# Moving the first fold, the late gate-tile subtractions, one expert store and the score sign in a two-layer diffusion backbone

## What is computed

```python
# two of three mixers
z = v                                            # hyena: short convolution first, then twice
for o, gate in enumerate((x1, x2)):
    z = gate * bidirectional_long_conv(z, h_spec[:, o], skip[o])
# neighbourhood attention, 8 heads of 64
s_lat = einsum(q_rot, k_rot) * scale + bias      # bias = -1e30 outside the column window
s_ctx = einsum(q_plain, k_ctx) * scale
p = softmax(concatenate([s_lat, s_ctx]))
# experts (top 2 of 16)
out = sum_e gates[:, e] * (silu(h @ w_gate[e]) * (h @ w_up[e])) @ w_down[e]
```

## Time and profile before

| | us |
|---|---|
| median of 3 runs | 1544.64 (1544.02 to 1546.52) |
| the profiled execution | 1546.05 |
| its span | 1544.3 |
| TensorE (matmul) busy in the span | 1447.1 (94%) |
| VectorE busy | 869.9 (56%) |
| ScalarE busy | 634.5 (41%) |
| GpSimd busy | 404.3 (26%) |

### The profile page before, as it was taken

One profiled execution on the slowest core, in us unless ns is written; L12 is line 12 of the kernel. 1 busy time (PEld: TensorE's weight loads), 2 busy tenths in 40 slices (PEclk: granted clock), 3 DMA queues, 4 the chain that ended last, 5 costly groups with the idle time before them and its releaser, 6 DMA issues. The chain is left out here.

```text
span 1544.3 us, 20627 instructions
## 1 busy us (share of the span) xinstructions
PE 1447.1 (94%) x8184; PEld 1080.0 (70%) x8184; DVE 869.9 (56%) x1265; ACT 634.5 (41%) x862; POOL 404.3 (26%) x367
## 2 busy tenths in 40 slices
PE   6999999899999997899999988989988997999997
PEld 2688788557778875688888854787958995545444
DVE  7626576763223347899999956465873565111112
ACT  3432321364223225588787836432264443010102
POOL 1455443201334520111111012564305670000000
PEclk9999999999999998999999999999999999999998
DMA  9422211475544544899999986342305776899993
GB/s 361 150 82 82 83 55 63 169 273 206 172 139 141 195 174 171 302 406 418 415 414 412 402 293 246 104 150 82 103 22 175 240 259 260 340 421 421 420 421 154
DMA packets 117186, 362.78 MB, mean 235 GB/s; under 512 B 7806, under 2 KB 73664, under 8 KB 86496
## 3 DMA queue, kind: packets, MB, share of 16 engines
q1 hardware_dynamic: 109584, 334.62, 56.9%
q0 software_dynamic: 7504, 26.81, 4.7%
HBM read 349.86 MB, written 11.53 MB: 234 GB/s over the span
## 5 line engine op out<-in xcount | busy, mean ns | idle before, releaser
L911 POOL TENSOR_TENSOR w_lo<-ring,w_hi 128x256 fp32r<-128x256 f32 (+1 forms) x300 | 345.7, 1182 | 497.5 <-ACT w_hi L1962 466.0
L1101 PE MATMUL bank<-h_hi,w_hi 128*128 128x512 f32 (+1 forms) x768 | 271.5, 353 | 8.6 <-POOL w_lo L911 2.9
L1103 PE MATMUL bank<-h_lo,w_hi 128*128 128x512 f32 (+1 forms) x768 | 263.1, 343 | 0.0
L1102 PE MATMUL bank<-h_hi,w_lo 128*128 128x512 f32 (+1 forms) x768 | 263.1, 343 | 0.0
L1101 PEld LDWEIGHTS bank<-h_hi,w_hi 128*128 128x128 f32 x768 | 146.6, 191 | 35.6 <-issue 9.5
L1102 PEld LDWEIGHTS bank<-h_hi,w_lo 128*128 128x128 f32 x768 | 146.7, 191 | 17.2 <-issue 1.4
L1103 PEld LDWEIGHTS bank<-h_lo,w_hi 128*128 128x128 f32 x768 | 146.5, 191 | 16.8
L1101 PE MATMUL bank<-w_hi,h_hi 128*128 128x512 f32 (+1 forms) x384 | 140.2, 365 | 7.1 <-DVE h_lo L2911 3.1
L1962 ACT ACTIVATE w_hi<-ring 128x1024 fp32r<-128x1024 f32 x120 | 125.3, 1053 | 43.5 <-PE bank L1101 29.8
L1103 PE MATMUL bank<-w_lo,h_hi 128*128 128x512 f32 (+1 forms) x384 | 136.9, 356 | 0.0
L1102 PE MATMUL bank<-w_hi,h_lo 128*128 128x512 f32 (+1 forms) x384 | 136.8, 356 | 0.0
(11 more groups left out here) (369 smaller groups left out, 2835.8 us busy)
## 6 DMA issues: line engine op xcount, KB each, us to landing
ring<-in_w_in SPq DMA_DIRECT2D x52, 1024.0 KB, 5.3
mix<-in_w_gate_e SPq DMA_DIRECT2D x40, 1024.0 KB, 8.2
ring<-in_w_up_e SPq DMA_DIRECT2D x38, 1024.0 KB, 8.1
mix<-in_w_down_e SPq DMA_DIRECT2D x25, 1024.0 KB, 8.3
ring<-in_w_down_e SPq DMA_DIRECT2D x23, 1024.0 KB, 8.1
ring<-in_w_mod SPq DMA_DIRECT2D x19, 1024.0 KB, 5.6
operands_plain<-in_w_up_e SPq DMA_DIRECT2D x16, 1024.0 KB, 12.6
operands_plain<-in_w_down_e SPq DMA_DIRECT2D x16, 1024.0 KB, 15.8
```

The lines of the kernel that those rows point to most:

```text
L911: last = pool.tensor_tensor(w_lo[:, slot, k:k + n], rview(raw, 8)[:, k:k + n, x * P:(x + 1) * P], w_hi[:, slot, k:k + n].bitcast(F32), ALU ...
L1101: first = mm(dst, stat[0], mov[0], start=start, stop=False)
L1102: mm(dst, stat[1], mov[0], start=False, stop=False)
L1103: return first, mm(dst, stat[0], mov[1], start=False, stop=stop)
```

## The change

Five edits, named A to E here.

**A, first fold.** The fold of the first of the transforms is issued on VectorE ahead of the pooling windows and goes to `ahead`, a buffer that is free then. TensorE transposes it ahead of the pooling products. ScalarE scales three of the four pooling products, then copies the transposed fold to `zt` (after a wait for the last pooling window, whose scratch it overwrites), then scales the fourth. The first transform waits for each scaled product on its own.

**B, sign of the scores.** ScalarE writes `qT` with the scale negated, so scores come negated. The exponential takes `scale=-1.0`, the column mask is +1e30, `mask_bias` subtracts the bias from the mask. `maxes` takes, for a unit with bias, first two minima over the 256 context columns (one for each head), and then for each head one `tensor_tensor_reduce` over the 256 latent columns, which adds the bias, stores the sum and folds the minimum in one operation.

**C, late subtractions.** GpSimd waits for the whole rotation (`r_d` at 8) before the subtraction of the last gate tile in layer 0 and of the last two in layer 1. In layer 0 the two before that one stand ahead of the first bias loads and of the wait for the last transform that these have.

**D, last store.** The last expert's rows are stored by ScalarE's queue with a semaphore of its own, `x_last`, right after ScalarE has written them. What waited for all stores waits for this one too.

**E.** Bookkeeping of the overflow branch, which is not taken, follows D.

```diff
@@ -267,7 +267,10 @@
-        hy_f = work[:, 3072:4096].rearrange("p (i c u) -> p i c u", i=2, c=BK)
+        def hy_f(n):
+
+            v = ahead[:, 0:1024] if n == 0 else work[:, 3072:4096]
+            return v.rearrange("p (i c u) -> p i c u", i=2, c=BK)
@@ -937,10 +941,20 @@
+                q = early
+                if l == 0:
+                    trail_ahead(q)
+                    trail_ahead(q + 1)
+                    q += 2
                 for c in range(BK):
                     if c == 2:
-                        for q in range(early, 2 * IN_C + AHEAD + PRE[l]):
+                        if l:
                             trail_ahead(q)
+                            q += 1
+
+                        pool.wait_ge(r_d[l], 8 * l + 8)
+                        for i in range(q, 2 * IN_C + AHEAD + PRE[l]):
+                            trail_ahead(i)
                     if c >= 2:
                         pool.wait_ge(a_mx[l], 2 * ((c - 2) * 2 * streams(l) + 2))
@@ -1005,16 +1019,17 @@
                 def all_stored():
-                    for i in range(2):
-                        pool.wait_ge(x_st[l][i], 16 * NS // 2)
+                    pool.wait_ge(x_st[l][0], 16 * NS // 2)
+                    pool.wait_ge(x_st[l][1], 16 * (NS // 2 - 1))
+                    pool.wait_ge(x_last, 16)
@@ -1302,26 +1317,33 @@
+                def fold_transposed(n):
+                    pe.wait_ge(y_fo[l], 8 * l + 2 * n + 2)
+                    for j in range(2):
+                        for c in range(BK):
+                            last = tp(bank[4 + j][:, c * P:(c + 1) * P], hy_f(n)[:, j, c, :], ident)
+                        last.then_inc(y_tp[l], 1)
+
+                fold_transposed(0)
                 for c in range(BK):
                     pe.wait_ge(j_d[l], 12 + c + 1)
                     mm(bank[c][:, 0:T], poolw[:, c, :], ypool[:, c, 0:T], start=True, stop=True
                        ).then_inc(pw_pe[l], 1)
 
-                pe.wait_ge(pw_a[l], 4 * l + BK)
...
                         for f in (0, 2, 1, 3):
+                            if n == 0:
+
+                                pe.wait_ge(pw_a[l], 4 * l + f + 1)
@@ -2025,17 +2047,26 @@
+                for c in range(BK - 1):
+                    pool_scaled(c)
+
                 for n in range(2 * S):
                     if n:
                         act.wait_ge(y_f[l], 16 * l + 4 * n)
+                    else:
+
+                        act.wait_ge(j_d[l], 12 + BK)
                     for j in range(2):
                         act.wait_ge(y_tp[l], 8 * l + 2 * n + j + 1)
                         A(zt[:, j, :], bank[4 + j][:, :], ACT.Copy).then_inc(y_zt[l], 1)
+                    if n == 0:
+                        pool_scaled(BK - 1)
@@ -2253,6 +2284,13 @@
+                if l == 0:
+
+                    act.wait_ge(x_ya[l], 16 * l + NS)
+                    act.wait_ge(x_yd[l], 16 * l + NS)
+                    act.dma_start(y_rows[l][(NS - 1) * P:NS * P, :], yb[:, (NS - 1) % 2, :]
+                                  ).then_inc(x_last, 16)
@@ -2520,6 +2558,16 @@
+                def fold(n):
+                    s = n % S
+                    early = hv[:, :, s * SEQ + P - 1:s * SEQ - 1 if s else None:-1]
+                    late = hv[:, :, s * SEQ + P:(s + 1) * SEQ]
+                    V.tensor_tensor(hy_f(n)[:, 0], late, early, ALU.add).then_inc(y_fo[l], 1)
+                    V.tensor_tensor(hy_f(n)[:, 1], late, early, ALU.subtract).then_inc(y_fo[l], 1)
+
+                dve.wait_ge(j_d[l], 12)
+                fold(0)
+
                 link(V.memset(up[:, :, 0:POOL_PAD], 0.0))
@@ -2618,19 +2662,25 @@
-                            link(V.tensor_tensor(b[:, 0:SEQ].rearrange("p (s j) -> p s j", s=4),
-                                                 b[:, 0:SEQ].rearrange("p (s j) -> p s j", s=4),
-                                                 bias[:, c % 2, h, k0:k0 + 4, :], ALU.add))
                         if v >= 2:
                             dve.wait_ge(a_nm[l], 2 * (v - 2) + h + 1)
-                        V.tensor_reduce(pstat[:, p, 0:1], b[:, 0:w], AX.X, ALU.max, negate=True).then_inc(a_mx[l], 1)
+                        if s == 0:
+                            V.tensor_reduce(pstat[:, p, 3:4], bank[p][:, SEQ:NT], AX.X, ALU.min).then_inc(dve_c, 1)
+                            chain[0] += 1
+                        else:
+                            V.tensor_reduce(pstat[:, p, 0:1], bank[p][:, 0:SEQ], AX.X, ALU.min).then_inc(a_mx[l], 1)
+                    if s:
+                        return
+                    k0 = 2 - 2 * x
+                    for h in range(2):
+                        p = 2 * (v % 2) + h
+                        dve.wait_ge(dve_c, chain[0] - 1 + h)
+                        V.tensor_tensor_reduce(bank[p][:, 0:SEQ], bank[p][:, 0:SEQ],
+                                               bias[:, c % 2, h, k0:k0 + 4, :].rearrange("p s j -> p (s j)"), 1.0,
+                                               pstat[:, p, 3:4], ALU.add, ALU.min, pstat[:, p, 0:1]).then_inc(a_mx[l], 1)
```

More of the change, by code:

```diff
@@ L466, in build @@
         x_st = [sems("expert_out_stored", 2)] * DEPTH
+        x_last = sem("last_expert_out_stored")
         v_w = sems("over_gate_up_loaded")
@@ L996, in _ @@
                     gather_rows(1)
-                for s in range(NS + 1):
-                    if s < NS and l == 0:
+                for s in range(NS):
+                    if l == 0:
                         if s == 0:
@@ L1007, in _ @@
                         store(s - 1)
-                    if s == NS - 1 and l == 0:
-                        pool.wait_ge(q_ix[l], l + 1)
-                        pool.wait_ge(x_st[l][0], 16 * NS // 2)
-                        pool.wait_ge(x_st[l][1], 16 * (NS // 2 - 1))
-                        first_choice(didx_early, (NS - 1) * P)
+                if l == 0:
+                    pool.wait_ge(q_ix[l], l + 1)
+                    pool.wait_ge(x_st[l][0], 16 * NS // 2)
+                    pool.wait_ge(x_st[l][1], 16 * (NS // 2 - 1))
+                    first_choice(didx_early, (NS - 1) * P)
                 def all_stored():
-                    for i in range(2):
-                        pool.wait_ge(x_st[l][i], 16 * NS // 2)
+                    pool.wait_ge(x_st[l][0], 16 * NS // 2)
+                    pool.wait_ge(x_st[l][1], 16 * (NS // 2 - 1))
+                    pool.wait_ge(x_last, 16)
                 def second_choice(rows):
@@ L1316, in _ @@
                             pe.wait_ge(y_z[l], BK * n)
-                        pe.wait_ge(y_fo[l], 8 * l + 2 * n + 2)
-                        for j in range(2):
-                            for c in range(BK):
-                                last = tp(bank[4 + j][:, c * P:(c + 1) * P], hy_f[:, j, c, :], ident)
-                            last.then_inc(y_tp[l], 1)
+                            fold_transposed(n)
                         fill_steps(plan[3 * n + 1])
@@ L2014, in take_tiles @@
                         if g < 20:
-                            A(qT[:, g - 16, 0:T], b[:, 0:T], ACT.Copy, scale=DH ** -0.5).then_inc(j_a[l], 1)
+                            A(qT[:, g - 16, 0:T], b[:, 0:T], ACT.Copy, scale=-DH ** -0.5).then_inc(j_a[l], 1)
                         elif g < 24:
@@ L2027, in _, with pool_scaled @@
                 take_tiles(at_start)
-                for c in range(BK):
+                def pool_scaled(c):
                     act.wait_ge(pw_pe[l], 4 * l + c + 1)
@@ L2052, in exps @@
                         p = 2 * (v % 2) + h
-                        A(prob[:, p, 0:w], bank[p][:, 0:w], ACT.Exp, bias=pstat[:, p, 0:1],
+                        A(prob[:, p, 0:w], bank[p][:, 0:w], ACT.Exp, scale=-1.0, bias=pstat[:, p, 0:1],
                           accum_out=pstat[:, p, 1:2]).then_inc(a_ex[l], 1)
@@ L2552, in _ @@
                     for s in range(S):
-                        early = hv[:, :, s * SEQ + P - 1:s * SEQ - 1 if s else None:-1]
-                        late = hv[:, :, s * SEQ + P:(s + 1) * SEQ]
-                        V.tensor_tensor(hy_f[:, 0], late, early, ALU.add).then_inc(y_fo[l], 1)
-                        V.tensor_tensor(hy_f[:, 1], late, early, ALU.subtract).then_inc(y_fo[l], 1)
                         if n:
+                            fold(n)
                             dve.wait_ge(y_i[l], 16 * l + BK * n)
@@ L2620, in maxes @@
                         dve.wait_ge(b_fix[l], BK * l + c + 1)
-                    w = NT if s == 0 else SEQ
                     for h in range(2):
@@ L2981, in _ @@
                     VP = 4 + l
-                    for i in range(2 if l == 0 else 0):
-                        dve.wait_ge(x_st[l][i], 128 * l + 16 * NS // 2)
+                    if l == 0:
+                        dve.wait_ge(x_st[l][0], 16 * NS // 2)
+                        dve.wait_ge(x_st[l][1], 16 * (NS // 2 - 1))
+                        dve.wait_ge(x_last, 16)
                     dve.wait_ge(v_tab[l], 2)
```

(2 more changed lines are left out.)

7 lines of the change are left out of this document (2 added, 5 removed).

## The result

| | median us | runs, us | ratio to the kernel before beside it, 95% interval |
|---|---|---|---|
| changed kernel, first set | 1527.6 | 4, 1526.1 to 1528.0 | 0.9897 [0.9877, 0.9917] |
| changed kernel, second chip | 1529.4 | 6, 1526.0 to 1532.4 | 0.9919 [0.9901, 0.9937] |
| changed kernel, third set | 1530.5 | 6, 1527.5 to 1532.6 | 0.9926 [0.9906, 0.9946] |
| kernel before, the same sets | 1544.3, 1542.0, 1540.5 | 4, 17, 11 | |

The forecast was 1530.0 us, range 1524 to 1538, 14.6 us gained. The sets give 16.7, 12.6 and 10.0 us. Each time is the median of that set's executions. The profiled execution of the changed kernel took 1526.1 us, the fastest of its set, with a span of 1524.4, 19.9 less than before. So the total is known to within some microseconds only. The terms can be read far more closely, since one event in two traces says by how much everything up to it moved.

The account below looks back on a forecast made before the run. TensorE, busy 94% of the span, bounds the kernel, so its removed gaps count. Terms 2.2 + 2.5 + 2.8 + 3.7 + 2.7 + 0.3 + 0.4 = 14.6 us take the median from 1544.64 to 1530.0; range 1524 to 1538.

Parts of the forecast that it names:

- A, layer 0: Mixers' start, layer 0: transform 8.5 us after the first transpose, near 161.0; gain 2.2 us, from 1.5 to 3.
- A, layer 1: Mixers' start, layer 1: fold ahead of the windows, transform at 1043.6 instead of 1046.1; gain 2.5, from 4 to loss 1.6.
- C and B, layer 0: Rotation and attention, layer 0: late subtractions net 2.8 us, maxima 0.3 because TensorE is the bound there.
- C and B, layer 1: Rotation and attention, layer 1: two TensorE gaps go, 3.7 us; cheaper maxima on VectorE give 2.7 us.
- D: End of layer 0: earlier store only clears VectorE's small work; gain 0.4 us, from 1.5 gained to 1 lost.
- C, layer 0: Layer 0 rotation ends 7.3 us earlier, 3.4 lost waiting for weights, 1.1 to low clock; net 2.8, from 0.5 to 6.
- The third piece: Modulation weights, layer 0: issued when a late gate tile ends, landing 7.7 us after the rotation; 3.4 goes back.
- C, layer 1: Layer 1 rotation: two late tiles leave, TensorE's gaps of 1.01 and 2.72 us go; gain 3.7, from 3 to 4.5.
- The rival of the late tiles that meet the scalings: Layer 1 attention: late subtractions delay probability scalings up to 2.4 us each, giving 1532 to 1534; chance 0.10.
- B, layer 1: Layer 1 attention: a unit with bias costs 1.8 us instead of 2.14 on VectorE; gain 2.7, from 4 to loss 2.
- The bound below: Combined operation in the attention: at least 0.33 us each, the pace of a 256-column reduction.
- The second choice: End of layer 0: comes some 7 us earlier, but covered by waits for the first choice; 0.4 us remains.

Follow-up runs that it names:

- C alone: Changed kernel with only the new sign of scores and maxima (B) undone, against the changed kernel: 1533.11 us, then 1533.64 us in a single execution.
- B alone: Changed kernel with only the late subtractions (C) undone, in both layers, against the changed kernel: 1533.8 us.

## Why the prediction was right, and where it wasn't

| term | predicted | measured, us | from |
|---|---|---|---|
| A, layer 0 | 2.2 | 1.7 to 2.2 | A undone, twice |
| A, layer 1 | 2.5 | 2.7 | A undone, twice |
| C and B, layer 0 | 2.8 + 0.3 | 3.2 to 3.5 (C alone 3.0, B alone 1.3) | shifts at 265 and 353 us |
| C and B, layer 1 | 3.7 + 2.7 | 7.4 (C alone 3.6, B alone 2.8) | shifts at 1112 and 1165 us |
| D | 0.4 | 0.0 to 0.9 | D undone |
| sum | 14.6 | 15.0 to 16.7 | |

The number was right, and so were the mechanisms of A, B and C; D's was not, and two sizes inside A and one in B were off. That it came within 2.4 us of the first median is partly luck: B gave 1.1 us more than its term, and the three sets spread over 6.7 us. Point by point:

- **A.** In layer 0 the transform came 8.2 us behind the first transpose (forecast 8.5). In layer 1 the fold went in front of the windows and was stretched, 2.92 and 2.89 us, each one turn of GpSimd's. The last products moved from a shift of -8.3 to -6.85, so they lost 1.5 (forecast 0.9), and the chain behind them took 5.4 us instead of the 5.9 of my sum (1037.7 to 1043.6): two misses that cancel, which is luck.
- **C, layer 0.** The rotation gave 7.5 us (shift -2.2 to -9.7; forecast 7.3). The third piece was there 7.7 us after the first scores (285.33 to 293.05), to the tenth what the sum had, and TensorE waited 3.87. Its eight matmuls then took 1.93 us at the low clock, and by 320 us 4.6 of the gain had gone back (shift -5.1; forecast 3.4 + 1.1). What I left out is that the pieces behind it land one after another, about 3 us apart: moving the third one's use gained nothing, moving its issue gained 4.
- **C, layer 1.** Both gaps went, 1.01 and 2.72 us, and 4.1 us were gained by the first scores (forecast 3.7), with one rotation instruction stretched, to 2.50 us, as forecast. The rival of the late tiles that meet the scalings missed by one microsecond, 1112.12 to 1113.09. The combined operations ran beside these tiles at their usual 0.48 us, and a pair of minima at its usual 0.76. By the Trainium skill, "SBUF — State Buffer", section "Who interferes with whom", a VectorE instruction with at most one SBUF input, outside the two-port modes, doesn't contend with GpSimd. The trace agrees.
- **B, layer 1.** The mis-sized step is the combined operation, 0.57 us in the sum and 0.40 from start to start in the trace. The bound below, 0.33, was nearer than the one I took: the accumulator's read of 0.14 us runs beside the next operation, where I had added it up. With 0.40 a unit comes to 1.48 us instead of 1.8, and B on top of C to 3.8 instead of 2.7.
- **D.** The second choice was covered, as forecast. The gain came by another way than I said. The step that failed is that D only clears VectorE's small work: with the store gone from behind the gathers, the first choice itself landed 1.1 us sooner, and TensorE's gap was 4.78 us, not near 6. The clock took most of it back.
- **What nobody forecast:** 1.7 us at the start of layer 1 and 0.5 us just before it that no single edit carries, and the clock of the last 30 us. They make the profiled execution's 19.9. In the other direction, the two later sets gave 12.6 and 10.0 us, less than the terms' sum. The kernel before was itself faster there, 1542.0 and 1540.5 us, and without traces of those executions I can't say where. That stays open.

## What to carry to other kernels

Before a tile is moved out of a stage's way, look at what hangs on its end: here it freed a slot of the weight ring, and the wait until the stage was over sent the next transfer out 7.8 us later (288.17 instead of 280.37). One tile beside the stage, with the small loads ahead of it in the queue, cost 0.9 us in the rotation and left the kernel 4 us ahead. When a gap is filled from elsewhere and comes back at a later consumer, the producer's row of transfers is the bound; here only an earlier first issue helped.

## What the runs showed of the hardware

- How long VectorE is held by GpSimd depends on what stands in the stream, not only on its length. Twelve pieces of 128 by 256 in a row held two instructions 2.56 and 3.55 us; four such pieces held two instructions 0.85 us each. Why VectorE got in after one piece here and after three or more there is not settled.
- With the same gaps in front, the same 63 or 64 matmuls near the end of one program took 9.57 us at a granted clock of 0.80 or 12.08 us at 0.56 in two executions. Near 600 us the same stretch took 29.99 us at 0.89 or 32.58 us at 0.84 in two kernels that do the same there. A difference of 3 us between two profiles of this kernel says nothing unless the shift is followed event by event.
- The last 1024 KB piece of layer 0's modulation weights, issued about 5.3 us ahead of where TensorE would take it, landed after 6.9 us in two of the 14 profiles, which made the wait of 1.5 us, and after 5.2 to 5.6 us in the others. The two kernels that showed it didn't show it again.
